# Early loads in the front, norm and u stages, and an earlier decay layer in the project stage, of a one-core RWKV-7 / S5 layer

## The chip, the cores and the metric

The kernel runs on one core of one Trainium2 chip. The metric is the device time of one execution in microseconds. Beside it stands one profiled execution, whose span and rows are what the text reads. TensorE is PE in the rows, VectorE DVE, ScalarE ACT, GpSimd POOL; SP is the engine that issues every DMA of this kernel.

## What is computed

One layer for 1152 tokens: 1024 noisy latent tokens on a grid and 128 context tokens, width 1024. What matters here, in the reference's words cut down:

```python
xs = x_sample + grid_pos_embed(n_tok, D_MODEL)            # row half: 512 columns, column half: 512 columns
h = rms_norm(x, norm1_g) * (1.0 + sc1) + sh1              # sc1, sh1 from silu(cond) @ w_ada + b_ada
z = h @ w_in                                              # r, k, v, wd, ad, gd, u
logw = -softplus(-(decay_base + einsum('btdr,drc->btdc', tanh(wd), w_decay_up))) - 0.5
a = sigmoid(iclr_base + einsum('btdr,drc->btdc', ad, w_iclr_up))
y_s, s_re, s_im = s5_mix(z[..., OFF_U:], ...)             # 32 groups of 16 channels, two directions
y_r, s_r = rwkv7_mix(z, ...)                              # 8 heads x 64, two directions
```

The row half of the position embedding is the same for 64 tokens in a row: a block of 128 tokens has two distinct rows of 512 numbers. Its column half is the same for every block.

## The kernel before, in words

The program is a row of stages, each a block with its own order written out by hand for each engine; between two stages all engines meet, and `clear` resets the semaphores of the stage that ended. One SBUF arena holds everything; a stage takes its tiles from the arena's current position.

**Front** (`stage_front`) loads constants and the adaLN weights (four loads of 2 MB, `Modulation.load`), computes shift and scale for the first norm, and on DVE builds the tables of powers of the S5 part, one small instruction behind the other. Its last load is `M.wu`, the u columns of `w_in`, 2 MB.

**Norm 1** (`stage_norm1`) runs over nine blocks of 128 tokens. For block b: SP loads `xt[b % 4]` and the row half of the embedding; DVE adds the row half (L475) and the column half (L476); ACT squares with a sum (L418), then after POOL's power (L443) scales into `xn` (L431); PE transposes eight times 128x128 (L462); DVE applies scale and shift (`modulate`, L492, eight instructions); ACT rounds to bf16 (L424, `M.hi`); POOL subtracts for the low part (L450, `M.lo`). The program order matters: DVE runs `add(b + 2)` ahead of `modulate` of block b, and ACT runs `squares(b + 1)` ahead of the scaling of block b. ACT also rounds the u weights (L425, one instruction ahead of all blocks), and POOL takes their low part in four pieces behind blocks 0 to 3 (L454).

**u** (`stage_u`) multiplies for u, builds the S5 tables on DVE and sends them to DRAM (`s5_tab`, eight records of 1.6 MB). **S5** (`stage_s5`) starts with the loads of records 0, 1 and 2 (L716) and PE's turn of record 0 (L757).

**Project** (`stage_project`) makes three hidden blocks and then, for each of four column tiles ct, the blocks r, k and v (`project(lane(ct, n))`, 72 bf16 matmuls of 384 columns, three for each product). Between them stand 21 small "pieces" on two PSUM banks in turn: `lora(ct, 0)`, the forward decay and learning-rate layers (six pieces), the bonus sums (L1206), the norm sums (L1209), the turn of v (L1215) and `lora(ct, 1)`. `bank` makes PE wait until ACT (L1235) or DVE (L1355) has read the piece that held the bank before. ACT reads the pieces in the same order. For ct over 0 it first waits for DVE's `x` of the tile before, empties the r block (L1231) and rounds the next weights (L1227):

```python
if ct:
    act.wait_ge(ev("x"), 8 * (ct - 1) + 4)
leave_bank(lane(ct, 0), r[ct % 2])
high(lane(ct, 2))
decays(ct, 0)
```

Of the kernel before, what the change touches and what calls it, by code (L numbers as in the profile page):

```python
# [8 lines left out]
F32 = mybir.dt.float32  # L9
# [6 lines left out]
D = 1024  # L16
KD = D // P
# [145 lines left out]
def stage_front(nc, M, ins):  # L163
# [7 lines left out]
    sc = M.silu  # L171
    wst = [A.take(KD, 512) for _ in range(2)]
# [10 lines left out]
    with ExitStack() as ctx:  # L183
# [5 lines left out]
        def _(sp):  # L189
# [12 lines left out]
            sp.dma_start(M.wu, ins["w_in"][:, :, OFF_U:OFF_U + DS]).then_inc(ev("w_u"), 16)  # L202
            sp.wait_ge(ev("w_u"), 16)
# [164 lines left out]
def stage_norm1(nc, M, ins):  # L368
# [4 lines left out]
    xt = [A.take(D) for _ in range(4)]  # L373
    rows = [A.take(D // 2) for _ in range(4)]
    columns = A.take(D // 2)
# [5 lines left out]
    with ExitStack() as ctx:  # L381
# [4 lines left out]
        def _(sp):  # L386
            def load(b):
                sp.dma_start(xt[b % 4], ins["x"][b]).then_inc(ev("loaded", b % 4), 16)
                if b < LB:
                    sp.dma_start(rows[b % 4], ins["pos"][b][:, 0:H]).then_inc(ev("loaded", b % 4), 16)  # L390
            load(0)
            sp.dma_start(columns, ins["pos"][0][:, H:D]).then_inc(ev("columns"), 16)
            for b in range(1, 4):
                load(b)
            for b in range(NB):
                if b < LB:
                    sp.wait_ge(ev("added"), 2 * b + 2)
                else:
                    sp.wait_ge(ev("loaded", b % 4), 32 * (b // 4) + 16)
# [9 lines left out]
        def _(act):  # L409
            def squares(b):  # L410
# [4 lines left out]
                else:  # L415
                    act.wait_ge(ev("loaded", b % 4), 32 * (b // 4) + 16)
# [8 lines left out]
            nc.scalar.activation(M.wu_hi, M.wu, ACT.Copy).then_inc(ev("wu_hi"), 1)  # L425
            squares(0)
            for b in range(NB):
# [4 lines left out]
                if b:  # L432
                    high(b - 1)
            high(NB - 1)

        @block.gpsimd
        def _(pool):
# [8 lines left out]
            for b in range(NB):  # L446
# [10 lines left out]
        def _(pe):  # L457
            for b in range(NB):
# [5 lines left out]
                last.then_inc(ev("transposed"), 1)  # L464

        @block.vector
        def _(dve):
            def add(b):
                if b >= LB:
                    return  # L470
                dve.wait_ge(ev("loaded", b % 4), 32 * (b // 4) + 32)
                if b == 0:
                    dve.wait_ge(ev("columns"), 16)
                x = xt[b % 4]
                nc.vector.tensor_tensor(x[:, 0:H], x[:, 0:H], rows[b % 4], ALU.add).then_inc(ev("added"), 1)  # L475
# [51 lines left out]
def stage_u(nc, M, ins):  # L527
# [13 lines left out]
    with ExitStack() as ctx:  # L541
# [5 lines left out]
        def _(sp):  # L547
# [20 lines left out]
            for i in range(G // PAIR):  # L568
# [3 lines left out]
                if i < 2:  # L572
                    mod.load(sp, i + 2)
            sp.wait_ge(ev("ada_row"), 2)
            sp.dma_start(ins["gates"][0], mod.rows[0:2, 0:D]).then_inc(ev("gates"), 16)
            sp.wait_ge(ev("gates"), 16)
            for q in range(2):
                sp.wait_ge(ev("rot_out", q), G // PAIR * 16)
                sp.wait_ge(ev("sent", q), G // PAIR * 32)

# [105 lines left out]
def stage_s5(nc, M, ins, outs):  # L686
# [22 lines left out]
    with ExitStack() as ctx:  # L709
# [4 lines left out]
        def _(sp):  # L714
# [8 lines left out]
            load(0)  # L723
# [26 lines left out]
        def _(pe):  # L750
            def turn(b):
                pe.wait_ge(ev("rec", b % 3), b // 3 * 16 + 16)
# [1896 lines left out]
```

## Time and profile before

| what | us |
|---|---|
| median of 3 runs | 2148.41 (2148.17 to 2150.22) |
| the profiled execution's own time | 2147.13 |
| its span | 2145.3 |
| front, about | 0 to 62.3 |
| norm 1, from the first instruction to the last | 62.3 to 118.8 |
| u | 119.9 to 228 |
| S5, from its first load | 230.8 to 396 |
| project | 476.2 to 769 |

Stages are separated by meetings of all engines, so the time of the program is the sum of what each stage takes, and inside a stage the engine or chain that ends last counts. A row gives the start in us from the span's start, the duration, engine, line and operation, and in brackets the idle time of that engine just before and who ended it.

### The profile page before, as it was taken

How to read it: one execution, taken by the hardware profiler on the slowest of the kernel's cores; microseconds unless marked ns; L12 is line 12 of the kernel's file. 1: busy time of each engine (PE TensorE's matmuls, PEld its weight loads, DVE VectorE, ACT ScalarE, POOL GpSimd, SP SyncE). 2: the span in 40 equal slices, each digit the busy share in tenths (PEclk: the TensorE clock that was granted, in tenths of full speed). 3: DMA queues.
4: the chain of work that ended last, by engine and by line, in shares of the span. 5: the costliest groups of instructions: out<-in, count | busy, mean ns of one | idle time of the engine just before them, and what ended most of it. 6: DMA issues, size and time to landing. Idle time of an engine off the chain costs nothing. (4 is left out here: it accounts for less than half of the span.)

```text
span 2145.3 us, 55493 instructions
## 1 busy us (share of the span) xinstructions
PE 1841.6 (86%) x24160; PEld 1152.4 (54%) x24160; DVE 1031.2 (48%) x1685; ACT 635.7 (30%) x1209; POOL 525.1 (24%) x596
## 2 busy tenths in 40 slices
PE   6289587779999648999999389799999999999988
PEld 1244476335555337999988244454545455454533
DVE  8789556510688834555544744222222222222276
ACT  0511244332555413444444213231203021120202
POOL 0510000033111023555544533231203111120110
PEclk9589689899999878999999699899999999999999
DMA  6664332421244354434343232221111121111122
GB/s 234 221 209 162 139 110 79 150 64 50 75 149 149 125 181 131 111 104 115 107 140 100 97 114 89 99 79 40 40 40 40 40 79 40 40 40 40 40 78 89
DMA packets 172361, 215.87 MB, mean 101 GB/s; under 512 B 41034, under 2 KB 127050, under 8 KB 170446
## 3 DMA queue, kind: packets, MB, share of 16 engines
q1 hardware_dynamic: 172244, 214.18, 30.5%
q8 instruction: 89, 1.46, 0.3%
q14 instruction: 28, 0.23, 0.0%
HBM read 151.63 MB, written 60.42 MB: 99 GB/s over the span
## 5 line engine op out<-in xcount | busy, mean ns | idle before, releaser
L89 PE MATMUL psum<-arena 128*128 128x384 bf16 (+1 forms) x2028 | 710.5, 350 | 71.4 <-PEq L500 14.7
L90 PE MATMUL psum<-arena 128*128 128x384 bf16 (+1 forms) x2028 | 709.6, 350 | 0.0
L91 PE MATMUL psum<-arena 128*128 128x384 bf16 (+1 forms) x2028 | 709.3, 350 | 0.0
L1629 PE MATMUL psum<-arena 64*64 64x64 f32 x9216 | 343.4, 224 | 24.5 <-issue 19.8
L89 PEld LDWEIGHTS psum<-arena 128*128 128x128 bf16 x2028 | 200.7, 99 | 267.0 <-issue 39.6
L1629 PEld LDWEIGHTS psum<-arena 64*64 64x64 f32 x9216 | 310.7, 136 | 43.0 <-issue 32.2
L1623 PE MATMUL psum<-arena 64*64 64x64 f32 (+2 forms) x6336 | 284.5, 239 | 47.7 <-DMA arena<-xrec 37.5
L91 PEld LDWEIGHTS psum<-arena 128*128 128x128 bf16 x2028 | 201.1, 99 | 178.3 <-issue 8.0
L90 PEld LDWEIGHTS psum<-arena 128*128 128x128 bf16 x2028 | 201.2, 99 | 171.1 <-issue 6.6
L1623 PEld LDWEIGHTS psum<-arena 64*64 64x64 f32 x6336 | 244.3, 136 | 53.4 <-issue 50.1
L1769 ACT ACTIVATE arena<-psum 128x192 f32<-128x192 f32 (+1 forms) x600 | 174.5, 337 | 267.8 <-PE psum L1629 191.4
L2434 DVE TENSOR_TENSOR arena<-arena 128x1152 f32<-128x1152 f32 x32 | 46.7, 1460 | 283.6 <-ACT arena L2336 283.6
L2404 DVE TENSOR_TENSOR arena<-arena,psum 128x512 f32<-128x512 f32 x108 | 73.5, 686 | 166.3 <-PE psum L91 166.3
L2303 POOL TENSOR_TENSOR arena<-arena 128x4096 bf16<-128x4096 f32 x8 | 63.6, 7950 | 308.4 <-ACT arena L2330 308.4
L2309 POOL TENSOR_TENSOR arena<-arena 128x1024 bf16<-128x1024 f32 x28 | 65.9, 2355 | 240.2 <-ACT arena L2322 240.2
L1560 POOL TENSOR_TENSOR arena<-arena 128x192 f32<-128x192 f32 x240 | 120.9, 533 | 7.2 <-PE psum L1629 7.0
L2336 ACT ACTIVATE arena<-psum 128x1152 f32<-128x1152 f32 x32 | 36.2, 1131 | 237.7 <-PE psum L91 237.7
L1880 DVE TENSOR_TENSOR arena<-psum,arena 128x192 f32<-128x192 f32 x240 | 76.9, 351 | 61.3 <-PE psum L1629 60.3
L2330 ACT ACTIVATE arena<-arena 128x4096 bf16<-128x4096 f32 x8 | 28.9, 3613 | 257.3 <-PE psum L91 257.3
L147 PE MATMUL psum<-arena 128*2 128x512 f32 x192 | 87.5, 608 | 2.0 <-DMA arena<-in_w_ada 2.0
L1150 POOL TENSOR_TENSOR arena<-arena 128x1024 bf16<-128x1024 f32 x15 | 35.3, 2352 | 153.4 <-ACT arena L1227 153.4
L1605 POOL TENSOR_TENSOR arena<-arena 128x192 f32<-128x192 f32 x48 | 24.3, 527 | 195.1 <-DVE arena L1892 195.1
(274 smaller groups left out, 2055.2 us busy)
## 6 DMA issues: line engine op xcount, KB each, us to landing
arena<-in_w_ff SPq DMA_DIRECT2D x16, 2048.0 KB, 7.8
arena<-in_w_ada SPq DMA_DIRECT2D x12, 2048.0 KB, 8.5
arena<-xrec SPq DMA_DIRECT2D x72, 320.0 KB, 3.4
arena<-s_tab SPq DMA_DIRECT2D x8, 1600.0 KB, 7.4
x<-arena SPq DMA_DIRECT2D x18, 512.0 KB, 3.4
xrec<-arena SPq DMA_DIRECT2D x4, 2304.0 KB
arena<-xrec SPq DMA_DIRECT2D x72, 128.0 KB, 2.6
arena<-x SPq DMA_DIRECT2D x18, 512.0 KB, 3.3
```

The source lines that it names most:

```text
L89: nc.tensor.matmul(out, whi, xhi, start=first, stop=False)
L90: nc.tensor.matmul(out, wlo, xhi, start=False, stop=False)
L91: return nc.tensor.matmul(out, whi, xlo, start=False, stop=last)
L147: last = nc.tensor.matmul(out, self.M.silu[:, k, :], self.wst[i % 2][:, k, :], start=False, stop=(k == KD - 1))
L1560: tt(lo[d][2 if l == 1 else l % 2], lt[d], wide3(M.level_mask[:, d, l]), ALU.mult).then_inc(ev("lo", l, d), 1)
L1623: done = nc.tensor.matmul(out[half[h]], lhs[half[h]], rhs[half[h]], start=first, stop=last)
L1629: done = nc.tensor.matmul(out[half[1 - h]], lhs[half[h]], rhs[half[h]], start=first, stop=last)
L1769: copy = lambda out, x: nc.scalar.activation(out, x, ACT.Copy)
L1880: tt(qs[d], ps[:, CROSS[d], 0:CHAIN].rearrange("p (j c) -> p j c", j=GROUP), wide3(M.ident64), ALU.add)\
L2303: nc.gpsimd.tensor_tensor(lo, w2s, hi, ALU.subtract).then_inc(ev("w2_lo"), 1)
L2309: nc.gpsimd.tensor_tensor(w1lo[:, :, cols], w1s[:, :, cols], w1hi[:, :, cols], ALU.subtract).then_inc(ev("w1_lo"), 1)
L2404: tt(a, a, ps[:, 6 + h, :], ALU.add).then_inc(ev("acc"), 1)
```

## The change

Four things.

1. Front: the adaLN weights go into `M.hi` and `M.lo`, which are still empty. Instead of the u weights, the front loads the first four blocks of x, the column half and, in place of eight row halves of 256 KB, two partitions (0 and 64) of a tile `M.pos_rows` of 8 x 512 words that POOL has set to zero with one memset.
2. Norm 1: the u weights are loaded as the stage's first DMA. The row half of block b is made by PE: `M.head_ones` (two 64x64 blocks of ones) times `M.pos_rows[:, b, :]`, an f32 matmul of 512 columns into PSUM bank 4 or 5, from where DVE adds it. PE makes rows 0 and 1 first, and row b + 2 behind the transposes of block b. ACT rounds the u weights in four pieces in iterations 2 to 5; POOL takes the low parts behind blocks 3 to 6.
3. u: after the third part's tables SP waits for the last u product and loads record 0 for the S5 stage into the place of the u weights; the S5 stage loads records 1 and 2 only.
4. Project: for ct 1 to 3 `lora(ct, 0)` stands ahead of `project(lane(ct, 1))` instead of behind it.

```diff
 def stage_front
-    wst = [A.take(KD, 512) for _ in range(2)]
+    wst = [v.rearrange("p k t -> p (k t)").bitcast(F32)[:, 0:KD * 512].rearrange("p (k n) -> p k n", k=KD) for v in (M.hi, M.lo)]
-            sp.dma_start(M.wu, ins["w_in"][:, :, OFF_U:OFF_U + DS]).then_inc(ev("w_u"), 16)
-            sp.wait_ge(ev("w_u"), 16)
+            for b in range(4):
+                sp.dma_start(M.xt[b], ins["x"][b]).then_inc(ev("x"), 16)
+            sp.dma_start(M.columns, ins["pos"][0][:, D // 2:D]).then_inc(ev("x"), 16)
+            sp.wait_ge(ev("rows_zero"), 1)
+            for row in (0, 64):
+                sp.dma_start(M.pos_rows[row:row + 1], ins["pos"][0:LB, row:row + 1, 0:D // 2].rearrange("b r n -> r b n")).then_inc(ev("x"), 16)
+            sp.wait_ge(ev("x"), 16 * 7)
+        @block.gpsimd
+        def _(pool):
+            nc.gpsimd.memset(M.pos_rows, 0.0).then_inc(ev("rows_zero"), 1)
...
 def stage_norm1
-                if b < LB:
-                    sp.dma_start(rows[b % 4], ins["pos"][b][:, 0:H]).then_inc(ev("loaded", b % 4), 16)
-            load(0)
-            sp.dma_start(columns, ins["pos"][0][:, H:D]).then_inc(ev("columns"), 16)
-            for b in range(1, 4):
-                load(b)
+            sp.dma_start(M.wu, ins["w_in"][:, :, OFF_U:OFF_U + DS]).then_inc(ev("w_u"), 16)
...
-            nc.scalar.activation(M.wu_hi, M.wu, ACT.Copy).then_inc(ev("wu_hi"), 1)
...
+                if 2 <= b < 6:
+                    ks = slice(2 * b - 4, 2 * b - 2)
+                    act.wait_ge(ev("w_u"), 16)
+                    nc.scalar.activation(M.wu_hi[:, ks], M.wu[:, ks], ACT.Copy).then_inc(ev("wu_hi"), 1)
...
-                if b < 4:
-                    ks = slice(2 * b, 2 * b + 2)
-                    pool.wait_ge(ev("wu_hi"), 1)
+                if 3 <= b < 7:
+                    ks = slice(2 * b - 6, 2 * b - 4)
+                    pool.wait_ge(ev("wu_hi"), b - 2)
...
+            def rows(b):
+                if b >= LB:
+                    return
+                need(pe, ev("added"), 2 * (b - 2) + 1 if b >= 2 else 0)
+                nc.tensor.matmul(ps[:, ROWS + b % 2, :], M.head_ones, M.pos_rows[:, b, :], start=True, stop=True).then_inc(ev("rows"), 1)
+            rows(0)
+            rows(1)
...
                 last.then_inc(ev("transposed"), 1)
+                rows(b + 2)
...
+                dve.wait_ge(ev("rows"), b + 1)
-                nc.vector.tensor_tensor(x[:, 0:H], x[:, 0:H], rows[b % 4], ALU.add).then_inc(ev("added"), 1)
+                nc.vector.tensor_tensor(x[:, 0:H], x[:, 0:H], ps[:, ROWS + b % 2, :], ALU.add).then_inc(ev("added"), 1)
...
 def stage_u
+                if i == 2:
+                    sp.wait_ge(ev("product"), CH + 1)
+                    for q in range(2):
+                        sp.wait_ge(ev("sent", q), 32)
+                    sp.wait_ge(ev("rot_out", 0), 32)
+                    sp.dma_start(M.first_rec, ins["s5_tab"][0]).then_inc(ev("rec"), 16)
...
 def stage_s5
-            load(0)
...
 def stage_project
                 project(lane(ct, 0))
+                if ct:
+                    lora(ct, 0)
                 project(lane(ct, 1))
                 if ct == 0:
                     pe.wait_ge(ev("up_lo"), 1)
                     pe.wait_ge(ev("hidden_lo"), HIDDEN)
-                lora(ct, 0)
+                    lora(ct, 0)
```

On PE at the start of norm 1, before (L462 is one block's eight transposes):

```order
L462 MATMUL psum<-arena 128x128 [waits norm1_scaled]
L462 MATMUL psum<-arena 128x128 x7
L462 MATMUL psum<-arena 128x128 [waits norm1_scaled]
L462 MATMUL psum<-arena 128x128 x7
L462 MATMUL psum<-arena 128x128 [waits norm1_modulated,norm1_scaled]
L462 MATMUL psum<-arena 128x128 x7
```

and with the change (L475 are the transposes there, L468 is the row matmul):

```order
L468 MATMUL psum<-arena 128x512 x2
L475 MATMUL psum<-arena 128x128 [waits norm1_scaled]
L475 MATMUL psum<-arena 128x128 x7
L468 MATMUL psum<-arena 128x512 [waits norm1_added]
L475 MATMUL psum<-arena 128x128 [waits norm1_scaled]
L475 MATMUL psum<-arena 128x128 x7
L468 MATMUL psum<-arena 128x512 [waits norm1_added]
```

Behind each block's transposes stands the row matmul of the block two later.

On ACT in the same stage with the change, iterations 1 and 2 (L421 squares, L433 scaling, L427 rounding, L439 a piece of the u weights):

```order
L421 ACTIVATE arena<-arena 128x1024 [waits norm1_added]
L423 ACTIVATE arena<-arena 128x1 [waits norm1_squares]
L433 ACTIVATE arena<-arena 128x1024 [waits norm1_rstd]
L427 ACTIVATE arena<-arena 128x8x128 [waits norm1_modulated]
L421 ACTIVATE arena<-arena 128x1024 [waits norm1_added]
L423 ACTIVATE arena<-arena 128x1 [waits norm1_squares]
L433 ACTIVATE arena<-arena 128x1024 [waits norm1_transposed,norm1_rstd]
L427 ACTIVATE arena<-arena 128x8x128 [waits norm1_modulated]
L439 ACTIVATE arena<-arena 128x1024 [waits norm1_w_u]
```

The order of squares, scaling and rounding is that of before; only the piece of the weights is new behind them.

On PE at the end of the r block of column tile 1, before:

```order
L90 MATMUL psum<-arena 128x384
L91 MATMUL psum<-arena 128x384
L89 MATMUL psum<-arena 128x384 [waits proj_evac,proj_w_lo]
L90 MATMUL psum<-arena 128x384
L91 MATMUL psum<-arena 128x384
```

and with the change:

```order
L91 MATMUL psum<-arena 128x384
L89 MATMUL psum<-arena 128x384 [waits proj_piece_read]
L90 MATMUL psum<-arena 128x384
L91 MATMUL psum<-arena 128x384
L89 MATMUL psum<-arena 128x384 [waits proj_piece_read]
L90 MATMUL psum<-arena 128x384
L91 MATMUL psum<-arena 128x384
```

Where the k block began, PE now comes to pieces that each wait for a reader.

## Rows read from the trace of the kernel before

**Rows 1.** The page: busy time by engine, and two DMA issues (size, landing).

```profile
PE 1841.6 (86%) x24160; PEld 1152.4 (54%) x24160; DVE 1031.2 (48%) x1685; ACT 635.7 (30%) x1209; POOL 525.1 (24%) x596
...
arena<-in_w_ada SPq DMA_DIRECT2D x12, 2048.0 KB, 8.5
...
x<-arena SPq DMA_DIRECT2D x18, 512.0 KB, 3.4
```

**Rows 2.** Timeline of norm 1, its start and the first blocks, all engines.

```profile
62.34 3.62 ACT L425 ACTIVATE arena<-arena 128x4096 bf16<-128x4096 f32 x1 [15.64 <-PEq L500]
...
70.75 0.69 DVE L475 TENSOR_TENSOR arena<-arena 128x512 f32<-128x512 f32 x1 [0.93 <-DMA arena<-in_pos]
...
72.09 1.06 ACT L418 ACTIVATE arena<-arena 128x1024 f32<-128x1024 f32 x1 [0.84 <-DVE arena L476]
...
73.38 1.13 ACT L431 ACTIVATE arena<-arena 128x1024 f32<-128x1024 f32 x1
...
74.57 1.97 PE L462 MATMUL psum<-arena 128*128 128x128 f32 x8 [27.16 <-ACT arena L431]
...
76.58 2.64 DVE L492 TENSOR_SCALAR arena<-psum,arena 128x128 f32<-128x128 f32 x8 [1.67 <-PE psum L462]
```

**Rows 3.** Timeline of norm 1, its middle and its end, POOL, DVE and PE.

```profile
82.48 2.15 POOL L454 TENSOR_TENSOR arena<-arena 128x1024 bf16<-128x1024 f32 x1
...
82.89 2.29 DVE L475 TENSOR_TENSOR arena<-arena 128x512 f32<-128x512 f32 x1
...
104.06 1.97 PE L462 MATMUL psum<-arena 128*128 128x128 f32 x8 [3.29 <-ACT arena L431]
...
116.70 2.13 POOL L450 TENSOR_TENSOR arena<-arena 128x1024 bf16<-128x1024 f32 x1 [1.19 <-ACT arena L424]
```

**Rows 4.** Weight loads of f32 matmuls of 512 columns (L147), timeline of PEld.

```profile
414.14 0.13 PEld L147 LDWEIGHTS psum<-arena 128*2 128x2 f32 x1 [0.72 <-issue]
...
417.20 0.08 PEld L147 LDWEIGHTS psum<-arena 128*2 128x2 f32 x1 [0.35 <-issue]
```

**Rows 5.** Stretches: length, PE busy (instructions), granted clock, DMA share, GB/s.

```profile
412.80:416.00 3.20, 3.20 (x5) 0.51 0.94 345
...
806.00:808.00 2.00, 2.00 (x62) 0.50 1.01 411
...
628.00:630.00 2.00, 2.00 (x8) 0.50 0.85 201
```

**Rows 6.** The same of all engines, in norm 1 (PE, PEld, DVE, ACT, POOL, clock).

```profile
92.00:98.00 6.00, 1.97 (x8) 1.57 (x8) 6.00 (x13) 4.16 (x9) 6.00 (x4) 0.50 0.68 241
```

**Rows 7.** Timeline: DVE in the front, then a POOL memset and a DVE scale.

```profile
3.31 0.18 DVE L240 TENSOR_SCALAR arena<-arena 128x32 f32<-128x32 f32 x1 [0.28 <-DMA arena<-in_ssm_par]
...
476.16 1.06 POOL L1151 MEMSET arena<- 128x1152 f32 x1 [4.21 <-POOLq L500]
...
483.64 2.14 POOL L1157 TENSOR_TENSOR arena<-arena 128x1024 bf16<-128x1024 f32 x1
...
483.70 2.12 DVE L1300 TENSOR_SCALAR arena<-arena 128x16 f32<-128x16 f32 x1
```

**Rows 8.** Timeline: the start of the S5 stage, SP and PE.

```profile
230.78 1.29 SPq L716 DMA_DIRECT2D arena<-s_tab  x3
...
237.62 1.97 PE L757 MATMUL psum<-arena 128*128 128x128 f32 x8 [16.57 <-DMA arena<-s_tab]
```

**Rows 9.** Timeline of project, tile 1: ACT and PE around the first decay layers.

```profile
587.15 1.14 ACT L1231 ACTIVATE arena<-psum 128x1152 f32<-128x1152 f32 x1 [0.45 <-DVE arena L1326]
588.17 1.05 ACT L1227 ACTIVATE arena<-arena 128x1024 bf16<-128x1024 f32 x1
...
599.98 0.33 PE L89 MATMUL psum<-arena 64*128 64x384 bf16 x1 [0.18 <-ACT arena L1235]
```

**Rows 10.** Timeline of project: the third bonus piece of tiles 1 and 3.

```profile
617.08 0.59 PE L1206 MATMUL psum<-arena 128*128 128x384 f32 x1 [1.50 <-DVE arena L1355]
...
724.60 0.59 PE L1206 MATMUL psum<-arena 128*128 128x384 f32 x1 [0.58 <-DVE arena L1355]
```

More of the change, by code:

```diff
@@ L170, in stage_front @@
     th = A.take(KD, 2)
-    sc = M.silu
-    wst = [A.take(KD, 512) for _ in range(2)]
+    sc = M.silu[:, :, 0:2]
+    wst = [v.rearrange("p k t -> p (k t)").bitcast(F32)[:, 0:KD * 512].rearrange("p (k n) -> p k n", k=KD) for v in (M.hi, M.lo)]
     par = A.take(3, G)
@@ L372, in stage_norm1 @@
     keep = A.at
-    xt = [A.take(D) for _ in range(4)]
-    rows = [A.take(D // 2) for _ in range(4)]
-    columns = A.take(D // 2)
+    xt, columns = M.xt, M.columns
+    ROWS = 4
     junk = A.take(D)
@@ L398, in _ @@
                 else:
-                    sp.wait_ge(ev("loaded", b % 4), 32 * (b // 4) + 16)
+                    sp.wait_ge(ev("loaded", b % 4), 16 * (b // 4))
                 sp.dma_start(ins["x1"][b], xt[b % 4]).then_inc(ev("stored", b % 4), 16)
@@ L415, in squares @@
                 else:
-                    act.wait_ge(ev("loaded", b % 4), 32 * (b // 4) + 16)
+                    act.wait_ge(ev("loaded", b % 4), 16 * (b // 4))
                 need(act, ev("rstd"), b - 3)
@@ L470, in add @@
                     return
-                dve.wait_ge(ev("loaded", b % 4), 32 * (b // 4) + 32)
-                if b == 0:
-                    dve.wait_ge(ev("columns"), 16)
+                need(dve, ev("loaded", b % 4), 16 * (b // 4))
+                dve.wait_ge(ev("rows"), b + 1)
                 x = xt[b % 4]
-                nc.vector.tensor_tensor(x[:, 0:H], x[:, 0:H], rows[b % 4], ALU.add).then_inc(ev("added"), 1)
+                nc.vector.tensor_tensor(x[:, 0:H], x[:, 0:H], ps[:, ROWS + b % 2, :], ALU.add).then_inc(ev("added"), 1)
                 nc.vector.tensor_tensor(x[:, H:D], x[:, H:D], columns, ALU.add).then_inc(ev("added"), 1)
@@ L579, in _ @@
                 sp.wait_ge(ev("sent", q), G // PAIR * 32)
+            sp.wait_ge(ev("rec"), 16)
         @block.scalar
@@ L751, in turn @@
             def turn(b):
-                pe.wait_ge(ev("rec", b % 3), b // 3 * 16 + 16)
+                need(pe, ev("rec", b % 3), (b + 2) // 3 * 16)
                 need(pe, ev("strip"), 2 * b)
@@ L882, in _ @@
                 cos, sin = (rot[b % 3][:, n].unsqueeze(1).broadcast_to([P, 2, QUAD * NC_]) for n in range(2))
-                dve.wait_ge(ev("rec", b % 3), b // 3 * 16 + 16)
+                need(dve, ev("rec", b % 3), (b + 2) // 3 * 16)
                 dve.wait_ge(ev("x"), 2 * b + 2)
@@ L2497, in program @@
     M.wu_hi, M.wu_lo = A.take(KD, DS, dt=BF16), A.take(KD, DS, dt=BF16)
+    M.first_rec = M.arena.t[:, keep_u + CH * DS:keep_u + CH * DS + S5_REC]
+    after_u = A.at
+    M.xt = [A.take(D) for _ in range(4)]
+    M.columns, M.pos_rows = A.take(D // 2), A.take(LB, D // 2)
     stage_front(nc, M, ins)
     stage_norm1(nc, M, ins)
+    A.at = after_u
     stage_u(nc, M, ins)
```

## The prediction, written before the changed kernel was timed

> **What bounds the kernel now.** I read the page first: PE is busy 86% of the span [rows 1], but a share over the whole program says little where stages meet at a barrier, so each edit is priced inside its stage. Then the timelines of the four stages, and the stretches with the granted clock. In norm 1 PE is nearly idle: in the six microseconds from 92 to 98 it works 1.97, while DVE and POOL work 6.00 each, and the granted clock is 0.50, that is 1.2 GHz [rows 6]. The start of that stage waits for loads: the stage begins at 62.34, and the first transposes start only at 74.57 [rows 2]. The S5 stage begins with a wait for its first record: issue at 230.78, PE at 237.62 [rows 8]. The project stage is PE's: its matmuls follow one another nearly without gaps, and the exceptions are short waits for a bank [rows 9, 10]; after its last PE instruction DVE has a fixed tail, so what PE loses before the last bonus piece moves the end of the stage one for one.
>
> **Front.** The u weights leave and the x blocks come in about the same bytes; the last transfer is issued around 31 and the stage ends by DVE's chain near 61, so the loads hide (2 MB land in 8.5 us [rows 1]). New is a POOL memset of 4096 words. The memset of 1152 took 1.06 us [rows 7], so 4096 take at most 3.8, less a fixed part about 3.5, and it runs from about 0.8 to 4.3. DVE's chain begins inside that time, with the scale at 3.31 [rows 7]. No row shows a memset against a DVE scale. The nearest is the scale of 16 columns that took 2.12 us while POOL had a subtraction of 2.14 [rows 7]: it stood until POOL was done. Taken over, the DVE chain starts about 1.2 us late; if a memset doesn't hold it, 0. A gain is excluded, nothing leaves that chain. I take +1.2, since the only scale that met POOL waited.
> The Trainium skill, page "SBUF — State Buffer", section "SBUF: two separate sides", says that a DVE operation in a two-port mode and any GpSimd operation exclude each other for a whole instruction, while one with two SBUF inputs is held only against GpSimd reads. By that rule the scales wait for the memset too, and the term is the same 1.2; no run here has shown it for a memset.
>
> **Norm 1, the start.** With x there, the first event is PE's rows 0 and 1. An f32 matmul of 512 columns has two passes. At the clock 0.51 [rows 5] one pass takes 0.13 + 0.72 = 0.85 us, at full clock 0.43 [rows 4]. PE has been idle for 15 us, so the low clock holds: both rows take 4 x 0.85 = 3.4, with the drain 3.5, until 65.85. Then block 1 is added: 1.34 us from the add's start to ACT's squares (70.75 to 72.09), 1.29 from squares to scaling, 1.19 from scaling to the transposes, all from [rows 2]. First transposes: 65.85 + 1.34 + 1.29 + 1.19 = 69.7, against 74.57. That is 4.9 us gained. The rounding of the u weights, 3.62 us [rows 2], was hidden in ACT's wait and gains nothing; its four pieces of about 1 us now stand in ACT's idle time. The load of the u weights goes ahead of the x stores and of block 4's load; by 8.5 and 3.4 us [rows 1] block 4 is there before 80, ahead of its use near 89.
>
> **Norm 1, the loop.** Here the edit closes a ring that was open. Row b + 2 stands on PE behind the transposes of block b; the add of block b + 2 needs it; ACT's squares of b + 2 need the add, and stand ahead of the scaling of block b + 1; the transposes of b + 1 need that scaling; behind them stands row b + 3. Nothing in the ring can overlap. Its length at the low clock: transposes 1.97, row matmul 1.7 and about 0.1 of drain, add 1.34, squares 1.29, scaling 1.19, together 7.6 us [rows 2, 4]. Six turns (T(0) to T(6), rows 2 to 7) take 45.6. Before, the same distance was 104.06 - 74.57 = 29.5 [rows 2, 3], paced by POOL with rounds of 5.26 where it had the weights' low part and shorter ones else. So +16.1. Two more things. The second add of a block has two SBUF inputs. In the rows of before the first add took 2.29 instead of 0.69 when POOL's weight part (82.48 to 84.63) was running [rows 3]. With the change POOL's part for blocks 3 and 4 runs from 3.5 to 5.6 us after a block's transposes start and the second add wants to start at 4.4: about 1.1 us each for two turns, +2.2. The first add now reads PSUM, as L492 does, and such a one did not wait. And the last blocks have POOL's remaining weight part in the tail: +0.5 beside 14.8 (104.06 to 118.83, the end of the last L450 [rows 3]). Sum of norm 1: -4.9 + 16.1 + 2.2 + 0.5 = **+13.9**. Bounds: at full clock each turn is 1.0 + 0.95 + 3.82 = 5.8, and the second add then falls into POOL's ordinary part, up to 0.9 more on five turns; the stage is between 0 (no such collision) and +4.5 there. With the low clock throughout it is +13.9. I take the low clock. Evidence: the clock was 0.50 through norm 1 [rows 6] and stayed at 0.50 over a stretch of 2 us without any gap in PE [rows 5]; a turn has 3.8 us of PE work and then 3.8 us of nothing.
> The Trainium skill ("TensorE: Matmul & The Clock Gate", section "HAM oscillation — how this bites in real kernels") says that bursts of matmuls with waits between them start at the low clock each time. By it the sum stays 13.9, and the full-clock rival below would not happen.
>
> **S5.** Record 0 is issued in the u stage around its 80th microsecond, when the u products are done and the earlier tables long sent; SP then sits before sends that are due 6 us later, and a load of 1.6 MB is done by then. In S5 PE can begin at once: 237.62 - 230.78 = **-6.8** [rows 8]. Records 1 and 2 have one less ahead of them. Bounds: -6.8, and 0 if the load held up the u stage's end.
>
> **Project.** In tile 1 PE ends r at about 586.8: the decay pieces began at 599.98 - 1.33 and k is 72 matmuls of 0.165 before that. Now the decay pieces start there. Two fit in the two banks (1.0 us, to 587.8); the third waits for ACT's reading of the first. But ACT comes to it only after emptying r, which waited for DVE until 587.15, and after rounding the next weights until 589.2 [rows 9]; with the reading of 0.58, 589.8. PE stands 2.0 us, where it stood 0.18 before [rows 9]: +1.85 for each of three tiles, **+5.6**. Against it: DVE gets the log decays 12 us sooner and is free at the bonus pieces. Tile 3 shows that state: there the third bonus piece waited 0.58 instead of 1.50 [rows 10]. So -0.9 in tiles 1 and 2, 0 in tile 3: **-1.8**. Last the clock: from 628 to 630 PE ran at 0.50 [rows 5], shortly behind the second decay layers with their gap of 1.24; such a stretch of 3.4 us costs 1.7. The new gap of 2.0 among half-array matmuls resembles it, the bonus gap of 1.5 did not bring one. Between 0 and 3 x 1.7 = 5.1, I take half, **+2.5**, as one kind of gap did and one didn't. Project: +6.3, bounds 3.8 to 8.9.
>
> **Sum.** 1.2 + 13.9 - 6.8 + 6.3 = +14.6. The profiled execution took 2147.13 around a span of 2145.3; it would take 2161.7. The median of the three runs is 1.3 above it: 2148.41 + 14.6 = **2163.0**.
>
> **Rivals.** (a) *Full clock in the norm loop.* The row matmuls, unlike transposes alone, raise the clock; the ring is 5.8 to 6.7 us; norm 1 costs 4.5: 1.2 + 4.5 - 6.8 + 6.3 = +5.2, 2153.6. For it: 3.8 us without a gap in each turn. Against: 3.8 us of nothing behind it. (b) *The same without any collision and with no clock loss in project:* -6.8 + 0 + 3.8 = -3.0, 2145.4. It needs POOL to be elsewhere in each turn. (c) *Faster, the ring doesn't bind.* If the row matmul is ready when DVE wants it, the loop stays at POOL's pace and the start's 4.9 us stay; project gives only its 1.8: -4.9 - 6.8 - 1.8 = -13.5, 2134.9. The point where this decides is the ring's length: below about 5 us it is hidden. Against it: 3.82 us of ring are DVE and ACT alone [rows 2]; PE would have to do both parts in 1.2. (d) *The early record isn't early:* SP's wait or the transfer holds the u stage, the 6.8 are not gained: 2169.8. For it: three waits in front of SP's last sends. Against: all are long met by then.
>
> **How the numbers follow.** Chances: forecast 0.62, (a) 0.15, (b) 0.08, (c) 0.08, (d) 0.07. The forecast's own range, by project's bounds, the memset's 0 and some turns at the higher clock, is 2156 to 2168. For 8 in 10 the range takes in (a) with its bounds and most of (d), and leaves out (b) and (c): 2149 to 2170. About 0.2%, 4.3 us, is what a measurement of this kernel can tell from no change: faster is (c), 0.08; within it are (b) and a quarter of (a), 0.12; slower is the rest, 0.80.
>
> **What would show it.** In the profile after: the first transposes at about 70; then one block's transposes every 7.6 us with ACT waiting for DVE, DVE for the row matmul, and POOL, full before, with gaps; the clock at 0.50 there. PE's first turn in S5 right at the stage's start. In project a wait of PE of 2 us for ACT's L1235 ahead of each k block, third bonus waits of 0.6. It is wrong if the blocks follow in 5 to 6 us, or if the k blocks start without that wait because ACT has been released earlier than the rows of before say.

## The result and the profile after

The changed kernel takes **2167.44 us** (median of six runs, 2162.28 to 2171.37) against 2148.29 (2146.20 to 2153.82) for the kernel before, timed beside it. The ratio is 1.0094, with a 95% interval of 1.0079 to 1.0109. It is slower by about 19 us, where 14.6 were forecast. The profiled execution took 2162.28 around a span of 2160.5, which is 15.2 more than the span of before and the quickest of the six runs.

Lengths of the stages in both profiles, from the issue of each stage's first DMA (norm 1: to POOL's last instruction there):

| stretch | before | after | difference | forecast |
|---|---|---|---|---|
| front | 61.6 | 62.4 | +0.9 | +1.2 |
| norm 1 | 56.5 | 69.7 | +13.2 | +13.9 |
| from there to S5 | 112.0 | 113.0 | +1.0 | 0 |
| S5 | 168.5 | 155.2 | -13.3 | -6.8 |
| glu | 76.9 | 76.5 | -0.3 | 0 |
| project | 293.5 | 305.6 | +12.1 | +6.3 |
| recurrence to the end | 1375.6 | 1377.2 | +1.6 | 0 |

The page of the kernel after, its row for PE and the granted clock in 40 slices (tenths):

```profile
PE 1859.6 (86%) x24176; PEld 1153.5 (53%) x24176; DVE 1028.5 (48%) x1685; ACT 635.6 (29%) x1212; POOL 524.3 (24%) x597
...
PEclk9579699899999869999999689899999999999999
```

PE is busy 18.0 us longer than in [rows 1], for 16 instructions more, the passes of the eight row matmuls. By stage it is +13.5 in norm 1, where these stand, +8.7 in project for the same 1560 matmuls, and -5.6 in S5 for the same 1408.

**The front.** Timeline of the kernel after, DVE and POOL in the first 5 us (start, length, engine, line, operation):

```profile
0.75 3.51 POOL L212 MEMSET arena<- 128x4096 f32 x1 [0.29 <-POOLq L2616]
...
2.96 1.33 DVE L281 TENSOR_SCALAR arena<-arena 128x16 f32<-128x16 f32 x1
3.23 1.08 DVE L249 TENSOR_SCALAR arena<-arena 128x32 f32<-128x32 f32 x1
```

The memset ends at 4.26. Two scales that began during it end at 4.29 and 4.31, and the next one takes its usual 0.18 [rows 7]. Not every DVE instruction was held: one with two inputs from SBUF (L280), from 2.75 on under the same memset, took 0.17, against 0.18 in the kernel before. The front ends 0.9 later.

**Norm 1.** Timeline of the kernel after, one turn of the ring, then the later transposes. L475 are the transposes, L468 the row matmuls, L488 and L489 DVE's two adds, L421 and L433 ACT's squares and scaling:

```profile
70.52 1.97 PE L475 MATMUL psum<-arena 128*128 128x128 f32 x8 [3.84 <-ACT arena L433]
72.28 1.92 PE L468 MATMUL psum<-arena 128*128 128x512 f32 x2
...
74.23 0.69 DVE L488 TENSOR_TENSOR arena<-arena,psum 128x512 f32<-128x512 f32 x1 [6.22 <-PE psum L468]
...
75.56 1.06 ACT L421 ACTIVATE arena<-arena 128x1024 f32<-128x1024 f32 x1 [5.10 <-DVE arena L489]
...
76.85 1.13 ACT L433 ACTIVATE arena<-arena 128x1024 f32<-128x1024 f32 x1
...
78.03 1.97 PE L475 MATMUL psum<-arena 128*128 128x128 f32 x8 [3.84 <-ACT arena L433]
...
109.22 1.97 PE L475 MATMUL psum<-arena 128*128 128x128 f32 x8 [5.06 <-ACT arena L433]
...
117.72 1.97 PE L475 MATMUL psum<-arena 128*128 128x128 f32 x8 [4.82 <-ACT arena L433]
```

The parts of a turn are 3.71 on PE, 1.33 for the adds, 1.29 and 1.18, together 7.51. The six turns from 70.52 to 117.72 are 7.51, 7.52, 7.59, 7.58, 8.50 and 8.50. The two long ones hold the meetings of DVE's second add with POOL's weight part, L460:

```profile
104.02 2.14 POOL L460 TENSOR_TENSOR arena<-arena 128x1024 bf16<-128x1024 f32 x1
...
104.27 0.69 DVE L488 TENSOR_TENSOR arena<-arena,psum 128x512 f32<-128x512 f32 x1 [3.51 <-PE psum L468]
104.88 1.83 DVE L489 TENSOR_TENSOR arena<-arena 128x512 f32<-128x512 f32 x1
```

The first add reads PSUM and keeps its 0.69 under the same POOL instruction. The second has both inputs in SBUF and ends 0.55 after POOL's 106.16 (the other one, in the next turn, 0.54 after). The clock and the busy times of an early turn, by the view of stretches (PE, PEld, DVE, ACT, POOL, clock), show POOL at 2.67 of 8.00 us where it was at 6.00 of 6.00 [rows 6]:

```profile
76.00:84.00 8.00, 3.67 (x10) 2.10 (x10) 4.33 (x13) 3.94 (x6) 2.67 (x2) 0.50 0.59 198
```

**S5.** The first turn starts with the stage. Before, it waited 6.8 [rows 8]:

```profile
245.87 1.11 SPq L736 DMA_DIRECT2D arena<-s_tab  x2
...
245.91 1.30 PE L776 MATMUL psum<-arena 128*128 128x128 f32 x5 [11.31 <-PEq L513]
```

**Project.** Tile 1: ACT around the first decay layers (L1252 empties r, L1248 rounds weights, L1256 reads the decay pieces), the third piece on PE, and the third bonus piece:

```profile
588.74 1.13 ACT L1252 ACTIVATE arena<-psum 128x1152 f32<-128x1152 f32 x1 [0.45 <-DVE arena L1347]
589.76 1.05 ACT L1248 ACTIVATE arena<-arena 128x1024 bf16<-128x1024 f32 x1
590.71 1.04 ACT L1256 ACTIVATE arena<-psum,arena 128x384 f32<-128x384 f32 x2
...
591.34 0.33 PE L89 MATMUL psum<-arena 64*128 64x384 bf16 x1 [1.69 <-ACT arena L1256]
...
622.19 0.91 PE L1227 MATMUL psum<-arena 128*128 128x384 f32 x2 [0.58 <-DVE arena L1376]
```

Then the stretches behind that wait, two microseconds each:

```profile
588.00:590.00 2.00, 1.64 (x10) 0.59 (x8) 1.97 (x7) 1.55 (x5) 0.00 (x0) 1.00 0.14 51
...
592.00:594.00 2.00, 2.00 (x7) 0.74 (x6) 2.00 (x1) 1.23 (x3) 1.16 (x1) 0.50 1.02 348
...
598.00:600.00 2.00, 2.00 (x12) 1.11 (x11) 1.97 (x7) 0.00 (x0) 0.00 (x0) 0.82 0.52 150
```

PE waits 1.69 and is then nearly without a gap, but about 7 us of it run at 1.2 GHz: 7 matmuls per 2 us, and 12 and more when the clock is back. The decay layers are half-array matmuls: they use 64 of the array's 128 rows (64x384 in the rows), where the blocks r, k and v use all 128. Behind it the third bonus piece waits 0.58, no longer 1.50 [rows 10]. The same stands in tiles 2 and 3, with waits of 1.64 us and with the clock at 0.52 from 650 to 657 and from 708 to 715. Each such stretch costs half its length, about 3.4 us. Below, "lost clock" is (1 - granted clock) x length, summed over the one-microsecond stretches of a stage. For the project stage it is 28.6 before and 37.8 after.

### The profile page after: what moved, and what is told of

Read it like the earlier page. It is cut to its first block and busy times, and to the rows that moved or that the text cites. A ratio compares the mean times of both kernels' runs of the same rounds, so it can differ in the third digit from the quotient of the medians.

```text
span 2160.5 us, 55531 instructions
## 1 busy us (share of the span) xinstructions
PE 1859.6 (86%) x24176; PEld 1153.5 (53%) x24176; DVE 1028.5 (48%) x1685; ACT 635.6 (29%) x1212; POOL 524.3 (24%) x597
## 5 line engine op out<-in xcount | busy, mean ns | idle before, releaser
L89 PE MATMUL psum<-arena 128*128 128x384 bf16 (+2 forms) x2028 | 715.4, 353 | 75.8 <-PEq L513 14.7
L90 PE MATMUL psum<-arena 128*128 128x384 bf16 (+2 forms) x2028 | 714.7, 352 | 0.0
L91 PE MATMUL psum<-arena 128*128 128x384 bf16 (+2 forms) x2028 | 713.8, 352 | 0.0
L89 PEld LDWEIGHTS psum<-arena 128*128 128x128 bf16 (+1 forms) x2028 | 201.9, 100 | 274.3 <-issue 43.9
L91 PEld LDWEIGHTS psum<-arena 128*128 128x128 bf16 (+1 forms) x2028 | 202.4, 100 | 180.9 <-issue 12.1
L90 PEld LDWEIGHTS psum<-arena 128*128 128x128 bf16 (+1 forms) x2028 | 202.3, 100 | 173.2 <-issue 9.7
L1901 DVE TENSOR_TENSOR arena<-psum,arena 128x192 f32<-128x192 f32 x240 | 76.9, 350 | 64.4 <-PE psum L1650 63.7
L147 PE MATMUL psum<-arena 128*2 128x512 f32 x192 | 88.6, 615 | 1.6 <-DMA arena<-in_w_ada 1.6
```

The costliest lines, as they stand in the source:

```text
L89: nc.tensor.matmul(out, whi, xhi, start=first, stop=False)
L90: nc.tensor.matmul(out, wlo, xhi, start=False, stop=False)
L91: return nc.tensor.matmul(out, whi, xlo, start=False, stop=last)
L147: last = nc.tensor.matmul(out, self.M.silu[:, k, :], self.wst[i % 2][:, k, :], start=False, stop=(k == KD - 1))
L1901: tt(qs[d], ps[:, CROSS[d], 0:CHAIN].rearrange("p (j c) -> p j c", j=GROUP), wide3(M.ident64), ALU.add)\
```

## The experiments

All times are compared with runs of the kernel before on the same chip. Its median was 2145.83 beside the first four kernels, 2144.05 beside the next four and 2142.88 beside the last three.

### 1. Each half by itself

e1 is the kernel before with the decay layers moved:

```diff
 def project / tensor, per ct
+                if ct:
+                    lora(ct, 0)
                 project(lane(ct, 1))
                 if ct == 0:
                     pe.wait_ge(ev("up_lo"), 1)
                     pe.wait_ge(ev("hidden_lo"), HIDDEN)
-                lora(ct, 0)
+                    lora(ct, 0)
```

> The kernel before with the moved decay layers alone. Theory: the wait of 1.65 us ahead of the k block and the stretch of about 7 us at clock 0.50 behind it come together, so project costs its whole +12 of the profile after (stalls +4.9, bonus waits -1.8, clock about +9): 2160 us. Rival 1, the prediction's term: the low stretches there belong to that execution and half of them at most follow from the wait: +6, 2154 us. Rival 2: the moved layers by themselves cost nothing and the low clock was brought by the other edits: within 2 us of before.

Measured: 2156.85 us, ratio 1.0055 (1.0038 to 1.0072), or +11.0. The project stage is 306.1 us long, with 38.7 of lost clock. PE's wait is 1.68. The first theory holds: the moved layers alone bring the whole loss of the stage.

e2 is the change with the decay layers in their old place:

> The change with the decay layers where they were before; all of the earlier loads. Theory: the two halves add up, front +0.8, norm 1 +13.2, u +1, S5 between -6.8 and -13.3 as the one profile after had it: 2150 to 2157 us, and 2155 if S5's second part is a matter of clock phases. Rival: the loads are the larger part of the loss, S5 gives only 6.8 and project's low stretches appear here as well: 2160 us or more.

Measured: 2153.57 us, ratio 1.0049 (1.0030 to 1.0068), or +7.7. Norm 1 has the change's slow turns (69.5 us, for 69.7), S5 takes 154.0, and project 294.2 with 29.2 of lost clock. The two halves sum to 18.7, against 19.2 for the whole. No interaction shows, within the few microseconds that the intervals leave.

### 2. The ring of norm 1, opened in two ways

e3 gives the row matmuls four PSUM banks:

```diff
-                need(pe, ev("added"), 2 * (b - 2) + 1 if b >= 2 else 0)
-                nc.tensor.matmul(ps[:, ROWS + b % 2, :], M.head_ones, M.pos_rows[:, b, :], ...
+                need(pe, ev("added"), 2 * (b - 4) + 1 if b >= 4 else 0)
+                nc.tensor.matmul(ps[:, ROWS + b % 4, :], M.head_ones, M.pos_rows[:, b, :], ...
-            rows(0)
-            rows(1)
+            for b in range(4):
+                rows(b)
...
-                rows(b + 2)
+                rows(b + 4)
```

> The change with four PSUM banks for the row matmuls instead of two, so that row b + 4 stands behind the transposes of block b and no add waits for a fresh one; the decay layers stay moved. Theory: the ring of 7.6 us is what paces norm 1; opened, blocks follow in 4.5 to 5.3 us at POOL's pace and the stage falls from 69.7 us by 15 to 18 us: 2150 to 2152 us against 2167 of the change. Rival 1: PE at the low clock (transposes 1.97 and rows 1.7 in each turn) or the meetings of DVE and POOL pace it: half of that, 2159 us. Rival 2: the ring isn't the cause: 2167 us.

Measured: 2145.74 us, ratio 1.0008 (0.9988 to 1.0029). No difference from the kernel before shows, where the change was 19.2 slower. The stage itself is 20.5 us shorter than in the change, a little more than the 15 to 18 expected. Timeline of e3, POOL at the end of norm 1:

```profile
102.67 0.53 POOL L449 TENSOR_TENSOR arena<-arena 128x1 f32<-128x1 f32 x1
103.17 2.14 POOL L456 TENSOR_TENSOR arena<-arena 128x1024 bf16<-128x1024 f32 x1
105.28 2.13 POOL L460 TENSOR_TENSOR arena<-arena 128x1024 bf16<-128x1024 f32 x1
...
110.26 2.13 POOL L456 TENSOR_TENSOR arena<-arena 128x1024 bf16<-128x1024 f32 x1 [0.75 <-ACT arena L427]
```

POOL has its parts back to back again, and the stage ends at 112.39, 49.2 us after its start (69.7 in the change, 56.5 before). PE does the same row matmuls, and five of the nine groups of transposes still take the 1.97 of the low clock (the other four take 1.09), yet the turns with 1.97 are 3.9 to 4.5 us long as well. So neither the work on PE nor its clock was the limit by itself. The limit was the place of the row in the chain.

e6 keeps two banks and exchanges two lines of ACT's program in the change:

```diff
             for b in range(NB):
-                squares(b + 1)
                 act.wait_ge(ev("rstd"), b + 1)
                 need(act, ev("transposed"), b - 1)
                 nc.scalar.activation(xn[b % 2], xt[b % 4], ACT.Copy, scale=rs[b % 4]).then_inc(ev("scaled"), 1)
+                squares(b + 1)
```

> The change with one line of ACT's order in norm 1 exchanged: the scaling of block b ahead of the squares of block b + 1, instead of behind them; still two PSUM banks for the rows. Theory: the ring of 7.6 us per block is closed by exactly this order, because the scaling of b + 1 waits behind the squares of b + 2 and so for the row behind the transposes of b; with the exchange the same 7.6 us of steps span two blocks, POOL (2.1 to 4.8 us a block) sets the pace, and norm 1 falls from 69.7 us (63.2 to 132.9 on POOL) to 50 to 55, as with four banks (63.2 to 112.4): 2147 to 2150 us. Rival: with the lookahead gone each block waits for its own squares and its 1/rms on POOL, the turns stay above 6 us, and at most half is won: 2158 us.

Measured: 2148.93 us, one run. Norm 1 takes 54.7 us, inside the expected 50 to 55. Timeline of e6, the first four transposes, with turns of 3.4, 6.2 and 4.7 (then 6.4, 4.2, 6.4):

```profile
69.91 1.97 PE L475 MATMUL psum<-arena 128*128 128x128 f32 x8 [3.16 <-ACT arena L432]
...
73.29 0.93 PE L475 MATMUL psum<-arena 128*128 128x128 f32 x7
...
79.52 0.69 PE L475 MATMUL psum<-arena 128*128 128x128 f32 x4 [4.33 <-ACT arena L432]
...
84.22 1.09 PE L475 MATMUL psum<-arena 128*128 128x128 f32 x8 [1.45 <-ACT arena L432]
```

The ring is the one named in the prediction. It is cut by taking ACT's order out of it as well as by giving PE room: short and long turns now alternate, and the mean of six is 5.2, where it was 7.9. In this stage e6 stays 5.5 us behind e3. Three waits of ACT's scaling for POOL's 1/rms (0.66, 0.66 and 1.33) are a part of it. In the long turns another one stands there: ACT's rounding of the block before waits 1.17 for DVE, and the scaling comes behind it. How the 5.5 are shared out was not measured.

### 3. The two turns of 8.5 us

e11 is the change with POOL's weight parts behind blocks 6, 7, 7 and 8 instead of 3 to 6:

```diff
-                if 3 <= b < 7:
-                    ks = slice(2 * b - 6, 2 * b - 4)
-                    pool.wait_ge(ev("wu_hi"), b - 2)
+                for j in {6: (0,), 7: (1, 2), 8: (3,)}.get(b, ()):
+                    ks = slice(2 * j, 2 * j + 2)
+                    pool.wait_ge(ev("wu_hi"), j + 1)
```

> The change with POOL's four low parts of the u weights moved from blocks 3 to 6 to blocks 6 to 8, behind the last add. Theory: the two turns of 8.50 us fall to 7.5, since no second add meets a POOL part any more (1.83 and 1.60 us there become 0.69), and the last instruction of norm 1 on POOL is 2 to 4 us behind because of the parts at the end. Rival: the longer turns come from elsewhere (ACT's rounding pieces): they stay at 8.5.

Measured: 2168.27 us, one run. The turns are 7.52, 7.51, 7.53, 7.22, 7.58 and 7.59, and all second adds take 0.68 or 0.69. Timeline of e11, the place of the first meeting:

```profile
104.39 0.69 DVE L488 TENSOR_TENSOR arena<-arena,psum 128x512 f32<-128x512 f32 x1 [3.74 <-PE psum L468]
105.00 0.69 DVE L489 TENSOR_TENSOR arena<-arena 128x512 f32<-128x512 f32 x1
...
134.15 2.15 POOL L460 TENSOR_TENSOR arena<-arena 128x1024 bf16<-128x1024 f32 x1
```

So 0.9 us in each of the two turns was the meeting, and the rival (ACT's rounding pieces, still in their place) falls. The parts at the end cost more than that: POOL ends at 136.30, where it was 132.87.

### 4. Why project loses 12 us

e4 is e1 with one more exchange, on ACT in tiles 1 to 3:

```diff
+                if ct:
+                    decays(ct, 0)
                 leave_bank(lane(ct, 0), r[ct % 2])
                 high(lane(ct, 2))
-                decays(ct, 0)
+                if ct == 0:
+                    decays(ct, 0)
```

> The kernel before with the moved decay layers, and in tiles 1 to 3 ACT reads the six decay pieces before it empties the r block, so that the third piece is not waited for. Theory: the wait is the cause of both the stall and the low clock; without it the k block starts within 0.3 us of the second piece, the clock stays at full speed there and only the bonus waits' -1.8 is left: 2146.5 us. Rival: the low clock comes from the half-array matmuls standing between two blocks, wait or not: about 9 us of loss stay, 2156 us.

Measured: 2146.65 us, ratio 1.0002 (0.9985 to 1.0020). The wait ahead of the third piece is 0.25, the project stage 294.2, lost clock 32.1. The stretches of e4 at the decay layers of tile 1:

```profile
586.00:588.00 2.00, 1.75 (x11) 0.79 (x10) 1.97 (x7) 1.10 (x3) 0.00 (x0) 1.00 0.45 161
588.00:590.00 2.00, 1.81 (x11) 0.63 (x10) 2.00 (x3) 1.74 (x4) 0.00 (x0) 1.00 1.01 344
590.00:592.00 2.00, 2.00 (x15) 1.20 (x13) 2.00 (x2) 1.97 (x3) 0.00 (x0) 1.00 1.02 349
```

The wait is gone and the clock stays at 2.4 GHz there. Of the 12 us only 0.7 are left against the profile of before. The expected gain of 1.8 from the bonus waits didn't show, because 1.7 of clock more than before was lost behind the second decay layers in each of tiles 1 and 2 (low for 6.8 us instead of 3.4).

e10 takes only part of the wait away (ACT empties r, reads the decay pieces, then rounds):

> The kernel before with the moved decay layers; in tiles 1 to 3 ACT empties r first, then reads the decay pieces, and rounds the next weights behind them, so that the wait ahead of the k block is about 0.65 us instead of 1.68. Theory A, the low clock follows from the length of the wait: the three stretches of 3.4 us of lost clock are gone or halved, project 294 to 299 us. Theory B, any wait at this place brings them: project 303 us (306.2 with the wait of 1.68, 294.2 with 0.25).

Measured: 2154.57 us, one run; project 301.5. The waits were 0.75, 2.37 and 0.74 in tiles 1 to 3, since in tile 2 ACT itself was late. The stretches of 8 us behind them:

```profile
584.00:592.00 8.00, 7.93 (x29) 3.66 (x30) 7.89 (x7) 3.78 (x6) 2.99 (x1) 0.57 0.63 213
640.00:648.00 8.00, 7.81 (x38) 3.73 (x37) 7.90 (x6) 4.59 (x7) 2.57 (x1) 0.79 0.76 258
696.00:704.00 8.00, 7.82 (x28) 3.40 (x27) 7.90 (x7) 4.33 (x6) 2.44 (x1) 0.57 0.71 240
```

The two waits of 0.75 and 0.74 are followed by the full loss of 3.4, and the longest, 2.37, by 1.7. So the loss doesn't grow with the wait, and theory A falls. Theory B is right in two tiles of three. Why the longest was cheaper stays open.

e13 asks for the other ingredient. It is the kernel before, in its old order, and PE waits for ACT between the whole-array blocks r and k:

```diff
+                if ct:
+                    pe.wait_ge(ev("evac"), lane(ct, 0) + 1)
                 project(lane(ct, 1))
```

> The kernel before with its own order, and in tiles 1 to 3 PE waits ahead of the k block until ACT has emptied the r block, so that a wait of 1.3 to 1.5 us stands there among whole-array matmuls. Theory A, a wait of over a microsecond is enough for the low clock: again 3.4 us of lost clock in each of the three tiles, project 293.5 + 3 x 1.4 + 10 = 308 us. Theory B, it takes the half-array decay layers together with the wait: no low stretch there, project 293.5 + 4 = 298 us, clock loss about 28 us in the stage as before.

Measured: 2150.50 us, one run; project 300.7, lost clock 30.7. Waits of 1.28, 1.35 and 1.28 stand there. The stretches of e13 at the wait of tile 1 and behind it:

```profile
582.00:584.00 2.00, 0.72 (x6) 0.24 (x4) 1.97 (x3) 1.40 (x2) 0.00 (x0) 1.00 0.99 346
584.00:586.00 2.00, 2.00 (x14) 1.20 (x13) 2.00 (x3) 0.68 (x1) 1.24 (x1) 1.00 1.02 346
...
588.00:590.00 2.00, 2.00 (x15) 1.17 (x13) 1.90 (x2) 0.00 (x0) 0.00 (x0) 1.00 0.74 206
```

A wait of 1.3 us among whole-array matmuls brings no low clock at its place in any of the three tiles. The stage grows by 7.2: 3.9 of waits, and 3.4 of clock lost behind the second decay layers of tiles 0 and 2, where the clock is low for 6.8 us instead of 3.4. (The stage's lost clock grows by 2.1 only, as 1.2 less stands in the tail behind PE's last pieces, where the clock costs nothing.)

With e1, e4 and e10 the case is this. The first decay layers with a wait of 0.74 or more among them lost clock at all eighteen places looked at: 3.4 at each of the fifteen in the change, e1, e3, e6 and e11 and at two of the three in e10, 1.7 at the last. The same layers with waits of 0.25 or less lost 1.7 at one place (in e12, below) and none at the other twenty, those of the five kernels with the layers in the old place among them. A wait of 1.3 without the layers lost none at three, and the bonus waits of 1.50 to 1.58, which also stand between whole-array matmuls, lost none at 23. It takes both.

How much is lost is a different question, and here the waits don't answer it. The second decay layers have the same half-array matmuls and in every tile of every profile a wait of 1.23 or 1.24. Stretches of 8 us behind it, in tiles 0 and 1 of e13:

```profile
566.00:574.00 8.00, 7.82 (x28) 3.56 (x28) 7.90 (x5) 2.99 (x5) 0.00 (x0) 0.57 0.63 160
...
624.00:632.00 8.00, 8.00 (x41) 4.16 (x40) 7.86 (x6) 2.31 (x3) 0.00 (x0) 0.79 0.55 145
```

and in tile 2 of e5 (section 5):

```profile
669.00:677.00 8.00, 7.67 (x46) 4.10 (x47) 7.93 (x4) 3.86 (x7) 0.00 (x0) 1.00 0.75 192
```

In tiles 0 to 2 of the thirteen profiles, 39 places, the clock was low for 3.4 us at 29, for 6.8 us at six and not at all at four. What decides between these is open.

### 5. The early record

e5 is the kernel before with only the third part of the change, record 0 loaded in the u stage:

> The kernel before with one thing of the change, the first S5 record loaded during the u stage. Theory: it saves the wait at the start of S5 and nothing else, 6 to 7 us of the stage beside what the clock gives or takes; the rounds behind the first scatter by 1.7 us steps of lost clock in identical code (the S5 stage took 168.5, 163.3 and 167.6 us in three kernels with the same S5 code): about 2140 us, 0.9970 of before. Rival: the shift by itself makes the later rounds shorter, as the profile after had it (-13.3): 2133 us, 0.9940.

Measured: 2136.44 us, ratio 0.9971 (0.9955 to 0.9986), or -7.6. Timeline of e5, where PE starts the S5 stage (it begins at 231.20):

```profile
231.20 0.82 SPq L723 DMA_DIRECT2D arena<-s_tab  x2
...
231.23 1.94 PE L763 MATMUL psum<-arena 128*128 128x128 f32 x8 [11.19 <-PEq L500]
```

The S5 stages of all profiles, in two groups of identical code there:

| | lengths of the S5 stage | mean |
|---|---|---|
| record loaded in the stage (before, e4, e1, e13, e10) | 168.5, 167.6, 163.3, 163.2, 162.4 | 165.0 |
| record loaded early (after, e2, e5, e12, e11, e6, e3, e9) | 155.2, 154.0, 156.4, 157.2, 157.7, 158.4, 158.9, 159.9 | 157.2 |

The difference is 7.8. The pair of profiles that stood first, 168.5 and 155.2, has the longest of the first group and one of the shortest of the second, and made 13.3 of it. The rival, that the shift shortens the later rounds, falls: its 0.9940 lies outside e5's interval. The clock is part of the scatter. The stretch from the start of S5 to its end has a mean clock of 0.82 before and 0.87 in e1, with the same code.

```profile
230.78:399.29 168.51, 121.30 (x1408) 110.27 (x1408) 87.10 (x88) 63.32 (x152) 0.35 (x3) 0.82 0.29 93
```

The same row of e1:

```profile
230.75:394.07 163.32, 113.80 (x1408) 102.91 (x1408) 87.12 (x88) 63.27 (x152) 0.35 (x3) 0.87 0.30 96
```

PE needs 7.5 us less there for the same 1408 matmuls. The mean clock isn't all of it, for e13 and e10 have 0.82 and 0.83 and are as short as e1 (163.2 and 162.4). Where in the rounds the low clock stands may decide it; that was not looked into.

### 6. The losses mended

e9 has the early loads with four banks, the decay layers in their old place, and the memset split in two halves:

```diff
-            nc.gpsimd.memset(M.pos_rows, 0.0).then_inc(ev("rows_zero"), 1)
+            nc.gpsimd.memset(M.pos_rows[:, 0:LB // 2], 0.0).then_inc(ev("rows_zero"), 1)
...
+            nc.vector.memset(M.pos_rows[:, LB // 2:LB], 0.0).then_inc(ev("rows_zero"), 1)
             dve.wait_ge(ev("tanh"), 1)
```

> Earlier loads with four PSUM banks for the row matmuls, the decay layers where they were before, and the 4096-word memset at the start split between POOL and DVE, 2048 words each. Theory: both memsets end before DVE's first scale at 3.2, so no scale takes over 0.3 us there and the front ends at 61.5 instead of 62.4; norm 1 at 58 us, S5 at 155 to 159, project 293.5: 2134 us, 0.9945 of before. Rival 1: the DVE half takes longer than 2.4 us and the chain starts late all the same: 2135 us. Rival 2: what the parts gain one by one isn't kept in sum, because later stages lose it again to lower clock: 2141 us or more.

Measured: **2133.20 us, ratio 0.9946 (0.9930 to 0.9963)**, faster than both kernels. Timeline of e9, POOL and DVE at the start:

```profile
0.75 1.80 POOL L212 MEMSET arena<- 128x2048 f32 x1 [0.29 <-POOLq L2615]
...
1.25 1.76 DVE L278 MEMSET arena<- 128x2048 f32 x1 [1.25 <-PEq L2615]
2.93 0.11 DVE L281 SCALAR_TENSOR_TENSOR arena<-arena 128x16 f32<-128x16 f32 x1
3.08 0.17 DVE L282 TENSOR_SCALAR arena<-arena 128x16 f32<-128x16 f32 x1
```

No scale is held, and the last DVE instruction of the front starts at 61.17 (61.19 in the kernel before, 62.02 in the change). Front 61.6, project 291.8.

e12 is the whole change, decay layers moved, with the same two repairs and e4's order on ACT:

> The whole change, moved decay layers too, with its three losses mended: four PSUM banks for the rows, the memset split between POOL and DVE, and ACT reading the decay pieces before it empties r. Theory: with the wait gone the moved layers are neutral (the same three repairs with the layers in their old place gave 2133.2 us, and reading first on the kernel before gave 1.0002): 2134 us, 0.995. Rival: the layers in the new place help the bonus waits by 1.8 us and the clock allows it here: 2131 us.

Measured: 2132.25 us, ratio 0.9944 (0.9927 to 0.9961). With e9 it can't be told apart, so the layers' place is neutral once ACT reads them in time. Its project stage is 294.4, with waits of 0.25 ahead of the k blocks and 1.7 of clock lost behind one of them. The rival's 2131 lies inside the interval as well.

## Why the prediction was right, and where it was wrong

**Direction and mechanism of norm 1: right.** The forecast ring of 7.6 us was 7.51 to 7.59, its four parts within 0.1 of the rows it was built from [rows 2, 4], the first transposes stood at 70.52 (69.7 plus the front's 0.9), and the stage's +13.2 answers to +13.9. Two runs that cut the ring in different places (e3, e6) both brought the stage back to 49 to 55 us. The rival (a), full clock in the loop, had its conditions met once: the clock rose for some of the time between 97 and 107, one row matmul took 1.68 instead of 1.92, and it fell back; it shortened nothing, since the second add of that turn waited for POOL anyway. In e11, where POOL was not in the way, a row matmul of 1.55 went with a turn of 7.22 instead of 7.5. Rival (c) needed a ring under 5 us.

**The collision: right in kind, a little too dear.** Two turns with DVE's second add held, at 0.9 each instead of 1.1, shown by e11. The first add, reading PSUM, was not held, as forecast.

**The memset: right.** +0.9 against 1.2; it held the scales until it ended, at 4.26. The prediction set it at the scale that met POOL [rows 7], and e9 shows it gone when the memset is over by then. By the rule of the Trainium skill ("SBUF — State Buffer", section "SBUF: two separate sides") a DVE operation in a two-port mode and a GpSimd operation exclude each other for a whole instruction. The trace agrees, if the scales ran in such a mode: the two held ones took 1.33 and 1.08 instead of 0.18, and both ended within 0.05 us of the memset.

**S5: right at -6.8; about half of the profiles' -13.3 was scatter.** e5 measured -7.6 (its interval is 3 to 10), and the groups of profiles differ by 7.8.

**Project: the step that failed is the clock's term.** The wait was 1.64 to 1.69 instead of 2.0, so +4.5 for +5.6: ACT's reading of the first piece began at 590.71 and let PE go on at 591.34, while PE had come free only at 589.65, 0.3 later against the other steps than the working had it. The bonus waits gave the 1.8. The clock was set at half of 3 x 1.7, +2.5, on the grounds that one kind of gap brought a low stretch and another didn't. It was 3 x 3.4, that is +10.2. (The stage's lost clock grew by 9.2 only, 28.6 to 37.8. The missing 1.0 lies behind the second decay layers of tile 3: PE's last instruction came 1.0 sooner after them, and the end of the stage did not.) Both halves of the guess were off: each wait brought the low clock, and each stretch was twice as long as the one taken as its pattern (about 7 us instead of 3.4). The sum with the measured terms is 4.5 - 1.8 + 10.2 = 12.9, which is 0.8 above the 12.1 of the profile; e1's timing has 11.0. Up to the second decay layers of tile 3 PE's busy time grew by 9.8 and the stage by 11.9, so the clock is by far the largest term. The prediction had the right distinction in its hands, half-array matmuls beside the gap in one case and whole-array ones in the other, and weighed it as a coin. e10 and e13 show that it decides whether clock is lost. Why 3.4 were lost and not 1.7 stays open: behind the second decay layers one and the same wait cost 0, 1.7 or 3.4.

**The total.** That the two profiles differ by 15.2, close to the forecast 14.6, is luck: S5 came out 6.5 lower there and project 5.8 higher. The medians differ by 19.2. The measured 2167.4 lies inside the range of 2149 to 2170, near its upper end. With project at 12 instead of 6.3 the sum would have been +20.3, for this +19.2. The 1.0 from norm 1's end to S5, and 1.6 behind project, had no term; the second is within what the profiles of kernels with identical code there show (1374.1 to 1381.3 from the recurrence to the end).

## What to carry to other kernels

When an operand is moved from a DMA to an engine that stands in the loop, follow it once round: each instruction that waits in order behind another belongs to the ring, and its length, not anyone's busy time, is the pace. More buffers (here two) or an exchange of two lines cut it. A short wait has two prices, its own length and what the clock does after it: here 1.7 us of waiting among half-array matmuls cost 3.4 more, and shorter ones as much. And a stage that differs by 13 us between two profiles may have changed by 7: look at other runs with identical code there before explaining the rest.

## What was new about the hardware

- Among the first decay layers (half-array, 64 rows), waits of 0.74 to 1.69 us were followed at all seventeen places by about 7 us at a granted clock of 0.50, and a wait of 2.37 by 3.4 us. Among the second ones, a wait of 1.23 or 1.24 was followed by 3.4 us of it at 29 of 39 places, by 6.8 at six and by none at four. Waits of 1.28 to 1.58 between whole-array matmuls were followed by none at 26 places.
- A POOL memset holds DVE scales just as a two-input POOL operation does: 1.33 and 1.08 us for what takes 0.18. A DVE instruction with two SBUF inputs took its 0.17 under the same memset. A DVE memset of 2048 words (1.76) and a POOL memset of 2048 (1.80) overlapped by 1.3 us and were both over 2.3 us after the first began, so neither held the other.
- The S5 stage with the same instructions took 162.4 to 168.5 us in five profiles, and PE's busy time in it went from 113.8 to 121.3.
